# Feed-forward: the gated product goes to a spare PSUM bank, ScalarE writes its high part, VectorE its low part

## The chip, the cores and the metric

One core of a Trainium2 chip runs the whole program. Its engines run side by side and meet only through semaphores: TensorE (PE in the profile, its weight loads PEld), VectorE (DVE), ScalarE (ACT), GpSimd (POOL) and SyncE (SP), which issues most DMAs. SBUF is the memory that all engines read and write. PSUM has eight banks of 128 x 512 fp32 values; matmuls write there. The metric is the time of one execution on the device in microseconds (us), the median of several runs; lower is better.

## The reference

Two layers on 1024 tokens of width 1024, in float32. Each layer is a mixer (convolution and retention in layer 0, stick-breaking attention in layer 1) and a SwiGLU feed-forward, each behind a modulated RMS norm. The change touches the feed-forward alone:

```python
def swiglu(h, w_gate, w_up, w_down):          # w_gate, w_up: 1024 x 2816, w_down: 2816 x 1024
    return (jax.nn.silu(h @ w_gate) * (h @ w_up)) @ w_down

h = rms_norm(x, norm_ffn_g[l]) * (1 + sc2) + sh2
x = x + g2 * swiglu(h, ffn_w_gate[l], ffn_w_up[l], ffn_w_down[l])
```

## The kernel before

Every float32 product is made from two parts. A value is split into a high part (rounded to the type fp32r) and a low part (the value minus the high part), and `three` (lines 566, 571, 572) issues three matmuls: high by high, high by low, low by high. GpSimd splits the weights: per slab of 512 KB four `tensor_scalar` (L544) write the high part and four `tensor_tensor` (L548) the low part. The split of the activations is the work of VectorE, with ScalarE for the norms.

**The feed-forward** is done in 11 chunks (`CHUNKS`) of 256 hidden columns, once as phase `ffn0` (about 640 to 1395 us of the trace) and once as `ffn1` (about 2020 to 2730 us). Tokens are in two halves h of 512, hidden columns in two blocks f of 128. For each h, PE makes four steps of 24 matmuls, gate and up of f = 0 and gate and up of f = 1, into the four banks of `psG` in turn. Then it makes, for each h, eight down steps m of 6 matmuls, again into the four banks in turn. In `ffn0` a chunk ends with eight small matmuls (L617) for the modulation of layer 1.

**The hidden block (h, f)**, called `hidden(h, f)` here, comes between. ScalarE writes `sil`, the SiLU of the gate bank (L950, as all its activations). VectorE multiplies it with the up bank into `hid32` in SBUF (L1547; the trace calls it `hid`). Then `split` makes the high part by a copy with a cast (L1269, `hid_hi`) and the low part by a subtraction (L1271, `hid_lo`). In `ffn0`, `ada` follows after each hidden block: two more VectorE instructions of 128x512 (mostly L1283) that add up the next layer's modulation from a DMA'd piece of `ada_w`. After the last hidden block of a chunk, VectorE takes the 16 down steps: each is one instruction (L1563) that adds a bank of `psG` into `xT`, and so frees the bank.

**What orders it.** There is no scheduler: each engine's program is written out by hand, and the waits are on counters. Two of them matter. The down step m = 4 of half 0 writes the bank of m = 0, so it waits until VectorE's first L1563 has read that. The down steps of half 1 need `f_lo` of `hidden(1, 1)`. The last chunk of `ffn0` (`last_turn`) is written in another order, since the next norm begins in it: the gate and up of (h, f) = (1, 1) come after the down steps of half 0, VectorE does the norm's Newton step (L1320 to L1326) before `hidden(1, 1)`, and PE runs the f = 0 part of four down steps before it waits for `f_lo` of `hidden(1, 1)`.

`psO`, the bank that the change uses, holds the attention outputs in the mixer phases and is otherwise unused in the feed-forward, until the last chunk of `ffn1` turns the output there.

Of the kernel before, what the change touches and what calls it, by code (L numbers as in the profile page):

```python
# [21 lines left out]
F32 = mybir.dt.float32  # L22
F32R = mybir.dt.float32r
ALU = mybir.AluOpType
ACT = mybir.ActivationFunctionType
# [5 lines left out]
H = 512  # L31
# [16 lines left out]
SIL = 2  # L48
# [82 lines left out]
def build(nc, a):  # L131
# [4 lines left out]
    with ExitStack() as ctx:  # L136
# [4 lines left out]
        def at(name, off, shape, dt=F32):  # L141
            return nc.alloc_sbuf_tensor_at(name, [P] + shape, dt, offset=base + off)
# [35 lines left out]
        hid = [at("hid_hi", QO, [2, T], F32R), at("hid_lo", QO + 8 * KB, [2, T], F32R)]  # L178
        F0 = QO + 16 * KB
        sil = [at(f"sil{n}", F0 + 2 * KB * n, [H]) for n in range(SIL)]  # L180
        hid32 = at("hid32", F0 + 4 * KB, [H])
        ada_raw = [at(f"ada_raw{n}", QO + (37 + 4 * n) * KB, [KT // ADA_PIECES, ADA_COLS]) for n in range(2)]
        ada_acc = at("ada_acc", QO + 45 * KB, [4, P])

# [104 lines left out]
        r_ocp = sem("r_ocp")  # L289
        r_rs = sem("r_rs")  # L290
        r_on = sem("r_on")
        f_hi = [sem("f_hi0"), sem("f_hi1")]
        f_lo = [sem("f_lo0"), sem("f_lo1")]
        s_raw_cp = sem("s_raw_cp")
# [24 lines left out]
        def bank(phase, s):  # L319
            return s % PHASE_BANKS.get(phase, BANKS)  # L320
# [6 lines left out]
        def bank_wait(eng, phase, i, s):  # L327

            eng.wait_ge(bank_read[bank(phase, s)], uses(phase, i, s) + 1)
# [11 lines left out]
        def half(h):  # L341
            return slice(H * h, H * h + H)
# [61 lines left out]
        def final(i):  # L404
            return isinstance(i, int) and i == CHUNKS - 1
# [537 lines left out]
        def _(act):  # L943
# [5 lines left out]
            def fn(o, i_, f, **kw):  # L949
                return nc.scalar.activation(o, i_, f, **kw)  # L950

            def load_set(n):
                nc.scalar.add_instruction(mybir.InstLoadActFuncSet(name=nc.get_next_instruction_name(), act_func_set_id=n))
# [9 lines left out]
            def norm_squares(norm, h, x_wait, tiles_after=lambda m: ()):  # L963
                g = 2 * int(norm[-1]) + h
                for k in range(KT):
                    x_wait(h, k)
                    if KT * g + k >= 2:
                        act.wait_ge(n_add, KT * g + k - 1)
                    fn(n_sq[k % 2][:], xT[:, k, half(h)], ACT.Square).then_inc(n_sqd, 1)
                    for tile in tiles_after(k):  # L970
                        norm_hi(norm, 0, tile)

            def norm_root(norm, h):

                g = 2 * int(norm[-1]) + h
                act.wait_ge(misc_done, norm_misc(norm, h))
                if h:
                    act.wait_ge(n_ht, KT * g)
                fn(n_r[:], psM[:], ACT.Ln, bias=EPS).then_inc(n_rs, 1)
                act.wait_ge(n_rs, 2 * g + 1)  # L980
                fn(n_r[:], n_r[:], ACT.Exp, scale=-0.5).then_inc(n_rs, 1)
# [2 lines left out]
                norm_squares(norm, 0, x_wait)  # L984
                norm_second(norm, x_wait, lambda m: NORM_PLAN[1, m][1])

            def norm_second(norm, x_wait, tiles_after, after_squares=None, between=None):
                norm_root(norm, 0)
                norm_squares(norm, 1, x_wait, tiles_after)
                if after_squares:  # L990
                    after_squares()
                norm_root(norm, 1)
                for k in range(KT):
                    norm_hi(norm, 1, k)
                    if between and k == 3:
                        between()
# [84 lines left out]
            def reload(l, stg, x_free):  # L1081


                for n in range(16):
# [10 lines left out]
                    if n in (4, 11):  # L1095
# [2 lines left out]
                        m = 0 if n == 4 else 4  # L1098
                        act.dma_start(xT[:, m:m + 4], x_dram[m:m + 4].rearrange("k p t -> p k t")).then_inc(x_back, 16)

            def ffn_act(phase, squares=None):
                l = int(phase[-1])
                def body(i):
                    for h in range(NH):
                        for f in range(2):
                            s = gu_step(phase, i, h, 2 * f)
                            if squares and final(i) and (h, f) == (1, 1):
                                squares()
                            act.wait_ge(gemm_done, G(phase, i, s))

                            act.wait_ge(f_hi[l], 4 * i + (2 * h + f + 1))
                            fn(sil[f][:], psG[:, bank(phase, s)], ACT.Silu).then_inc(bank_read[bank(phase, s)], 1)
                load_set(SILU_SET)
                chunks(act, body)

# [11 lines left out]
            def qkv_first(phase, i, off, e, head):  # L1127

                hd = head[0] + i * head[1]
                s = 2 * off + e  # L1130
                act.wait_ge(gemm_done, G(phase, i, s))
                m, h, n = qkv_step(phase, e)
                if m < 2:

                    act.wait_ge(s_qk3, hd * 12 + 3 * n)
                    fn(s_raw[:], psG[:, bank(phase, s)], ACT.Copy).then_inc(bank_read[bank(phase, s)], 1)
                    bank_wait(act, phase, i, s)
                    fn(s_sq[:], s_raw[:], ACT.Square).then_inc(s_raw_cp, 1)
                else:

                    act.wait_ge(misc_done, M(phase, i, s) - 1)
                    fn(s_vsb[:], psG[:, bank(phase, s)], ACT.Copy).then_inc(bank_read[bank(phase, s)], 1)
# [64 lines left out]
            def head(phase, i, off, hd, hd_next, par):  # L1207
# [9 lines left out]
                for t in range(1, NT):  # L1217
# [2 lines left out]

            act.sem_inc(s_we, ZRING)
            norm_second("norm2", x_done, lambda m: FINAL_TILES.get(m, ()), lambda: spill("norm2", lambda: None),
                        lambda: qkv_first("qkv0", 0, 0, 0, (0, 0)))
            for e in range(6):
                if e:
                    qkv_first("qkv0", 0, 0, e, (0, 0))
# [29 lines left out]
        def _(dve):  # L1256
# [3 lines left out]
                dve.sem_inc(q, ONE)  # L1260
            dve.sem_inc(s_wst, 3)
            dve.sem_inc(s_wm, 2)
            dve.sem_inc(f_hi[0], SIL)
            dve.sem_inc(f_hi[1], SIL)
            dve.sem_inc(s_spb, 2)

            def split(o, i_, hi_sem, hi_n, lo_sem, add=None):
# [268 lines left out]
            def ffn_dve(phase, norm=None, gains=None):  # L1536
                l = int(phase[-1])
                def body(i):
                    last_one = bool(norm) and final(i)
                    def hidden(h, f):  # L1540
                            e = 2 * h + f
                            n = 4 * i + e
                            s = gu_step(phase, i, h, 2 * f + 1)
                            dve.wait_ge(gemm_done, G(phase, i, s))
                            bank_wait(dve, phase, i, s - 1)
                            dve.wait_ge(f_lo[l], ONE + n)
                            V.tensor_tensor(hid32[:], sil[f][:], psG[:, bank(phase, s)], ALU.mult).then_inc(bank_read[bank(phase, s)], 1)  # L1547
                            bank_wait(dve, phase, i, s)
                            split([q[:, f, half(h)] for q in hid], hid32[:], f_hi[l], n + 1 + SIL, f_lo[l])
                            if phase == "ffn0" and not final(i):  # L1550
                                ada(phase, i, e)
                    for h, f in ((0, 0), (0, 1), (1, 0)):
                        hidden(h, f)
                    if not last_one:
                        hidden(1, 1)
                    for h in range(NH):
                        for m in range(KT):
                            s = down_step(phase, i, h, m)
                            b = bank(phase, s)
                            dve.wait_ge(gemm_done, G(phase, i, s))  # L1560
                            if (h, m) == (1, KT - 1):
                                dve.sem_inc(slab_used, 1)
                            V.scalar_tensor_tensor(xT[:, m, half(h)], psG[:, b], mod[:, l * MOD + 5 * KT + m:l * MOD + 5 * KT + m + 1],  # L1563
                                                   xT[:, m, half(h)], ALU.mult, ALU.add).then_inc(bank_read[b], 1)
                            if last_one:
                                if m >= 2:
                                    norm.add(h, m - 2)
                                if h == 1:
                                    for k in FINAL_TILES.get(m, ()):
                                        norm.h_tile(0, k)  # L1570
                        if last_one:
                            norm.add(h, KT - 2)
                            if h == 0:
                                norm.add(0, KT - 1)
                                gains()
                                norm.newton(0)
                                hidden(1, 1)
                        if phase == "ffn0" and h == 1 and not final(i):
                            ada_cols(phase, i, 0, ada_cols_of(phase, i, 0))
                chunks(dve, body)  # L1580
                if norm:
                    norm.rest()
# [154 lines left out]
```

## Time and profile before

| | us |
|---|---|
| median of 3 runs | 2750.29 |
| lowest, highest | 2749.25, 2760.8 |
| span of the profiled execution | 2751.8 |
| PE busy | 2578.5 (94%) |
| DVE busy | 1377.9 (50%) |
| ACT busy | 543.2 (20%) |
| POOL busy | 973.7 (35%) |

The span is that of one profiled execution, from its first to its last instruction. Durations below come from it. A row of the timeline gives start, duration, engine, line, operation, what it writes and reads, and in brackets the idle time of the engine ahead of it with what ended that. Where rows of one kind follow each other they are merged, "x4" being four of them; a merged row's time runs from the first start to the last end. Since a VectorE instruction starts a little before the one ahead of it is through, starts are the better measure where instructions follow each other closely.

### The profile page before, as it was taken

How to read it: one execution, taken by the hardware profiler on the slowest of the kernel's cores; microseconds unless marked ns; L12 is line 12 of the kernel's file. 1: busy time of each engine (PE TensorE's matmuls, PEld its weight loads, DVE VectorE, ACT ScalarE, POOL GpSimd, SP SyncE). 2: the span in 40 equal slices, each digit the busy share in tenths (PEclk: the TensorE clock that was granted, in tenths of full speed). 3: DMA queues.
4: the chain of work that ended last, by engine and by line, in shares of the span. 5: the costliest groups of instructions: out<-in, count | busy, mean ns of one | idle time of the engine just before them, and what ended most of it. 6: DMA issues, size and time to landing. Idle time of an engine off the chain costs nothing.

```text
span 2751.8 us, 34959 instructions
## 1 busy us (share of the span) xinstructions
PE 2578.5 (94%) x11394; PEld 2103.1 (76%) x11394; DVE 1377.9 (50%) x2143; ACT 543.2 (20%) x987; POOL 973.7 (35%) x1604
## 2 busy tenths in 40 slices
PE   2999888599999999999989999997999999999999
PEld 2787777478888878887858888885778888888887
DVE  5636666546444444444367677777463333332223
ACT  3200111112000000000146666664120000000001
POOL 0432222514444434444322222224064433444430
PEclk7899999899999999999999999997999999999999
DMA  7233333431222222222120111113221111111111
GB/s 277 80 105 97 92 98 107 128 110 62 85 76 83 88 65 79 86 79 69 39 86 26 44 31 43 31 39 105 75 62 54 47 52 46 46 46 53 47 36 61
DMA packets 216925, 201.88 MB, mean 73 GB/s; under 512 B 5994, under 2 KB 165892, under 8 KB 216708
## 3 DMA queue, kind: packets, MB, share of 16 engines
q1 hardware_dynamic: 202708, 164.13, 19.5%
q10 hardware_dynamic: 14128, 36.70, 3.7%
q8 instruction: 38, 0.62, 0.1%
q14 instruction: 51, 0.42, 0.0%
HBM read 179.84 MB, written 20.97 MB: 73 GB/s over the span
## 4 chain that ended last, share of the span: by engine, by line
PE 84%; DVE 9%; DMA 3%; issue 2%; ACT 1%; POOL 1%; SPq 0%; DVEq 0%; ACTq 0%; POOLq 0%
PE psG L566 25%; PE psG L571 25%; PE psG L572 25%; PE psM L819 1%; DVE n_t L1344 1%; PE psG L860 1%; DMA o_stg<-o_spill 1%; PE psO L566 1%; DVE h_lo L1336 1%; PE psZ L849 1%; DMA w_raw<-in_ev_w_in 1%; DVE r_w L1497 1%; PE psO L571 1%; PE psO L572 1%; DVE r_wp L1271 1%
## 5 line engine op out<-in xcount | busy, mean ns | idle before, releaser
L566 PE MATMUL psG<-h_hi,w_split 128*128 128x512 f32 x2496 | 993.5, 398 | 52.1 <-DVE h_lo L1271 33.6
L571 PE MATMUL psG<-h_lo,w_split 128*128 128x512 f32 x2496 | 981.7, 393 | 0.0
L572 PE MATMUL psG<-h_hi,w_split 128*128 128x512 f32 x2496 | 980.8, 393 | 0.0
L544 POOL TENSOR_SCALAR w_split<-w_raw 128x256 fp32r<-128x256 f32 x800 | 368.8, 487 | 1703.5 <-PE psG L566 554.2
L548 POOL TENSOR_TENSOR w_split<-w_raw,w_split 128x256 fp32r<-128x256 f32 x800 | 613.1, 797 | 0.0
L566 PEld LDWEIGHTS psG<-h_hi,w_split 128*128 128x128 f32 x2496 | 474.6, 190 | 169.8 <-issue 34.4
L572 PEld LDWEIGHTS psG<-h_hi,w_split 128*128 128x128 f32 x2496 | 474.3, 190 | 101.2
L571 PEld LDWEIGHTS psG<-h_lo,w_split 128*128 128x128 f32 x2496 | 475.4, 190 | 97.8 <-issue 2.4
L1547 DVE TENSOR_TENSOR hid<-sil,psG 128x512 f32<-128x512 f32 x88 | 60.6, 688 | 720.4 <-PE psG L572 717.8
L1563 DVE SCALAR_TENSOR_TENSOR xT<-psG,mod,xT 128x512 f32<-128x512 f32 x352 | 259.7, 748 | 171.6 <-PE psG L572 171.4
L950 ACT ACTIVATE sil<-psG 128x512 f32<-128x512 f32 x88 | 52.5, 599 | 1307.1 <-PE psG L572 1307.1
L566 PE MATMUL psG<-hid_hi,w_split 128*128 128x512 f32 x704 | 276.6, 393 | 10.1 <-DVE xT L1563 9.9
L571 PE MATMUL psG<-hid_lo,w_split 128*128 128x512 f32 x704 | 275.4, 391 | 0.0
L572 PE MATMUL psG<-hid_hi,w_split 128*128 128x512 f32 x704 | 275.4, 391 | 0.0
L566 PEld LDWEIGHTS psG<-hid_hi,w_split 128*128 128x128 f32 x704 | 133.1, 189 | 40.4 <-issue 13.0
L572 PEld LDWEIGHTS psG<-hid_hi,w_split 128*128 128x128 f32 x704 | 133.0, 189 | 27.9
L571 PEld LDWEIGHTS psG<-hid_lo,w_split 128*128 128x128 f32 x704 | 133.1, 189 | 27.3
L1283 DVE SCALAR_TENSOR_TENSOR ada_acc<-ada_raw,c_act,ada_acc 128x512 f32<-128x512 f32 x140 | 116.0, 829 | 2.8
L950 ACT ACTIVATE s_z<-s_z 128x128 f32<-128x128 f32 (+2 forms) x192 | 100.8, 525 | 6.1
L950 ACT ACTIVATE n_sq<-xT 128x512 f32<-128x512 f32 x64 | 39.9, 630 | 192.6 <-DVE xT L1532 89.6
L1271 DVE TENSOR_TENSOR hid_lo<-hid,hid_hi 128x512 fp32r<-128x512 f32 x88 | 68.2, 775 | 3.0
L1271 DVE TENSOR_TENSOR s_w<-s_w,s_w 128x128 fp32r<-128x128 f32 (+2 forms) x96 | 64.1, 668 | 3.3
(160 smaller groups left out, 2103.2 us busy)
## 6 DMA issues: line engine op xcount, KB each, us to landing
ada_raw<-in_ada_w SPq DMA_DIRECT2D x80, 512.0 KB, 4.0
w_raw<-in_ffn_w_gate SPq DMA_DIRECT2D x44, 512.0 KB, 3.9
w_raw<-in_ffn_w_up SPq DMA_DIRECT2D x44, 512.0 KB, 3.9
w_raw<-in_ffn_w_down SPq DMA_DIRECT2D x44, 512.0 KB, 3.5
w_raw<-in_ev_w_in SPq DMA_DIRECT2D x28, 512.0 KB, 5.1
w_raw<-in_od_w_qkv SPq DMA_DIRECT2D x24, 512.0 KB, 3.8
ada_first<-in_ada_w SPq DMA_DIRECT2D x4, 2048.0 KB, 13.0
x_spill<-xT ACTq DMA_DIRECT2D x2, 4096.0 KB, 16.2
```

The lines of the kernel that those rows point to most:

```text
L544: nc.gpsimd.tensor_scalar(slot[:, 0, part], raw[:, part], 1.0, 1.0, ALU.mult, ALU.mult).then_inc(hi_done, 1)
L548: lo = nc.gpsimd.tensor_tensor(slot[:, 1, part], raw[:, part], slot[:, 0, part].bitcast(F32), ALU.subtract)
L566: mm = nc.tensor.matmul(o, st[0], mv[0], start=first, stop=False, **kw)
L571: nc.tensor.matmul(o, st[0], mv[1], start=False, stop=False, **kw)
L572: return nc.tensor.matmul(o, st[1], mv[0], start=False, stop=end, **kw)
L819: misc(phase, i, 2 * off + e, [lambda: nc.tensor.matmul(psM[:], ones_head, s_sq[:], start=True, stop=True)])
L849: mm = nc.tensor.matmul(zbank[t % ZRING][:, c0:], split_c[:, 1], s_s[:, t % SRING, n, c0:], start=False, stop=n == 1, skip_group_check=True)
L950: return nc.scalar.activation(o, i_, f, **kw)
L1271: V.tensor_tensor(o[1], i_, o[0].bitcast(F32), ALU.subtract).then_inc(lo_sem, 1)
L1283: V.scalar_tensor_tensor(acc, src, cc, acc, ALU.mult, ALU.add).then_inc(ada_step, 1)
L1547: V.tensor_tensor(hid32[:], sil[f][:], psG[:, bank(phase, s)], ALU.mult).then_inc(bank_read[bank(phase, s)], 1)
L1563: V.scalar_tensor_tensor(xT[:, m, half(h)], psG[:, b], mod[:, l * MOD + 5 * KT + m:l * MOD + 5 * KT + m + 1], xT[:, m, half(h)], ALU.mult, ...
```

## The change

The product is written to `psO` instead of `hid32`. ScalarE reads `psO` and writes the high part `hid[0]` with an activation of type Copy. VectorE waits for that and subtracts the high part from `psO`. The cast of VectorE and the buffer `hid32` are gone. A new pair of semaphores, `f_mul`, tells ScalarE of the product. The release of the up bank of `psG`, which the product gave itself, is now a semaphore instruction of VectorE after its wait for the high part. In the last turn of `ffn0`, ScalarE's copy of block (1, 1) stands after the two activations of the norm's root, since VectorE's product stands after the Newton step there. This holds for all 88 hidden blocks of both phases.

```diff
-        hid32 = at("hid32", F0 + 4 * KB, [H])
...
+        f_mul = [sem("f_mul0"), sem("f_mul1")]
...
                 norm_root(norm, 0)
+                if after_root:
+                    after_root()
...
+            def hid_high(l, i, h, f):
+
+                act.wait_ge(f_mul[l], 4 * i + (2 * h + f + 1))
+                fn(hid[0][:, f, half(h)], psO[:], ACT.Copy).then_inc(f_hi[l], 1)
+
...
                             act.wait_ge(gemm_done, G(phase, i, s))
-
-                            act.wait_ge(f_hi[l], 4 * i + (2 * h + f + 1))
                             fn(sil[f][:], psG[:, bank(phase, s)], ACT.Silu).then_inc(bank_read[bank(phase, s)], 1)
+                            if not (squares and final(i) and (h, f) == (1, 1)):
+                                hid_high(l, i, h, f)
...
-                        lambda: qkv_first("qkv0", 0, 0, 0, (0, 0)))
+                        lambda: qkv_first("qkv0", 0, 0, 0, (0, 0)), lambda: hid_high(0, CHUNKS - 1, 1, 1))
...
-            dve.sem_inc(f_hi[0], SIL)
-            dve.sem_inc(f_hi[1], SIL)
...
-                            V.tensor_tensor(hid32[:], sil[f][:], psG[:, bank(phase, s)], ALU.mult).then_inc(bank_read[bank(phase, s)], 1)
-                            bank_wait(dve, phase, i, s)
-                            split([q[:, f, half(h)] for q in hid], hid32[:], f_hi[l], n + 1 + SIL, f_lo[l])
+                            V.tensor_tensor(psO[:], sil[f][:], psG[:, bank(phase, s)], ALU.mult).then_inc(f_mul[l], 1)
+                            dve.wait_ge(f_hi[l], n + 1)
+                            dve.sem_inc(bank_read[bank(phase, s)], 1)
+                            V.tensor_tensor(hid[1][:, f, half(h)], psO[:], hid[0][:, f, half(h)].bitcast(F32), ALU.subtract).then_inc(f_lo[l], 1)
```

VectorE in the loop over the chunks of `ffn0`, the second hidden block of a chunk with its two `ada` instructions. Before:

```order
481 L1547 TENSOR_TENSOR hid_86<-sil_85,psG 128x512 [waits f_lo0]
482 L1269 CAST hid_hi<-hid_86 128x512 [waits bank_read3]
483 L1270 REGISTER_ALU
484 L1271 TENSOR_TENSOR hid_lo<-hid_86,hid_hi 128x512 [waits f_hi0]
485 L1282 ISA [waits ada_in1]
486 L1283 SCALAR_TENSOR_TENSOR ada_acc<-ada_raw_88,c_act,ada_acc 128x512 [waits ada_step]
```

After:

```order
475 L1552 TENSOR_TENSOR psO<-sil_85,psG 128x512 [waits f_lo0]
476 L1555 TENSOR_TENSOR hid_lo<-psO,hid_hi 128x512 [waits f_hi0]
477 L1287 ISA [waits ada_in1]
478 L1288 SCALAR_TENSOR_TENSOR ada_acc<-ada_raw_87,c_act,ada_acc 128x512 [waits ada_step]
479 L1287 REGISTER_ALU
```

The cast is gone, and the subtraction's wait for `f_hi0` is now one for ScalarE. (Lines behind the edit move by five to seven: L1283 becomes L1288.)

ScalarE in the last turn of `ffn0`, from the SiLU of block (1, 1) to the squares of the norm's second half. Before:

```order
195 L950 ACTIVATE sil_85<-psG 128x512 [waits f_hi0,gemm_done]
196 L953 ACT_TABLE_LOAD
197 L950 ACTIVATE n_r<-psM 128x512 [waits misc_done]
198 L950 ACTIVATE n_r<-n_r 128x512 [waits n_rs]
199 L950 ACTIVATE n_sq_76<-xT 128x512 [waits n_add,bank_read0]
```

After:

```order
206 L950 ACTIVATE sil_85<-psG 128x512 [waits gemm_done]
207 L953 ACT_TABLE_LOAD
208 L950 ACTIVATE n_r<-psM 128x512 [waits misc_done]
209 L950 ACTIVATE n_r<-n_r 128x512 [waits n_rs]
210 L950 ACTIVATE hid_hi<-psO 128x512 [waits f_mul0]
211 L950 ACTIVATE n_sq_76<-xT 128x512 [waits n_add,bank_read0]
```

The copy stands between the norm's root and the next squares, and everything of ScalarE behind it waits for VectorE's product.

## Rows read from the trace of the kernel before

**Rows 1.** The page, part 1: busy time, share of the span, instructions.
```profile
PE 2578.5 (94%) x11394; PEld 2103.1 (76%) x11394; DVE 1377.9 (50%) x2143; ACT 543.2 (20%) x987; POOL 973.7 (35%) x1604
```
**Rows 2.** By stretch: us, busy PE PEld DVE ACT POOL, granted clock, DMA share, GB/s.
```profile
1030.00:1033.00 3.00, 3.00 (x9) 2.35 (x8) 1.82 (x3) 0.00 (x0) 0.00 (x0) 0.51 0.94 294
2050.00:2725.00 675.00, 675.00 (x2980) 558.92 (x2979) 202.15 (x292) 24.57 (x41) 267.81 (x475) 1.00 0.15 45
```
**Rows 3.** Waits of PE, 700 to 1360 us: total us, times, longest.
```profile
PE psG L566 <- DVE xT L1563: 9.9, 3, 4.7
```
**Rows 4.** Chain that ended last, 700 to 1360 us: start, us, what.
```profile
708.57 0.79 PE psM L617 x8
...
908.38 0.79 PE psM L617 x8
...
974.61 0.79 PE psM L617 x8
...
1019.84 6.42 DVE hid_hi L1269
...
1047.45 0.79 PE psM L617 x8
...
1320.28 0.79 PE psM L617 x8
```
**Rows 5.** Timeline of DVE in the chunk that ends at 1047 us.
```profile
1019.12 0.69 DVE L1547 TENSOR_TENSOR hid<-sil,psG 128x512 f32<-128x512 f32 x1 [5.80 <-PE psG L572]
...
1026.29 0.69 DVE L1271 TENSOR_TENSOR hid_lo<-hid,hid_hi 128x512 fp32r<-128x512 f32 x1
1026.90 1.53 DVE L1283 SCALAR_TENSOR_TENSOR ada_acc<-ada_raw,c_act,ada_acc 128x512 f32<-128x512 f32 x2
1028.35 2.72 DVE L1563 SCALAR_TENSOR_TENSOR xT<-psG,mod,xT 128x512 f32<-128x512 f32 x4
```
**Rows 6.** Timeline of POOL there.
```profile
1023.17 2.80 POOL L548 TENSOR_TENSOR w_split<-w_raw,w_split 128x256 fp32r<-128x256 f32 x4
```
**Rows 7.** By tile, `hid`: duration in ns, min/median/max.
```profile
L1547 DVE TENSOR_TENSOR hid<-sil,psG x88: 682/689/691, 664.8 to 2716.5; 128x512 f32<-128x512 f32 x88
L1269 DVE CAST hid_hi<-hid x88: 426/428/6414, 665.5 to 2717.2; 128x512 fp32r<-128x512 f32 x88
```
**Rows 8.** By line, the nearest instructions to the new ones, min/median/max in ns.
```profile
L950 ACT ACTIVATE s_v<-psM x16: 597/599/600, 1430.8 to 1869.7; 128x512 fp32r<-128x512 f32 x16
...
L1611 DVE TENSOR_TENSOR s_v<-psM,s_v x16: 679/691/693, 1431.4 to 1870.7; 128x512 fp32r<-128x512 f32 x16
```
**Rows 9.** Timelines of ACT and DVE, a result that passes from ACT to DVE.
```profile
1403.12 0.63 ACT L950 ACTIVATE n_r<-n_r 128x512 f32<-128x512 f32 x1
...
1403.79 0.69 DVE L1320 SCALAR_TENSOR_TENSOR n_t<-psM,n_r 128x512 f32<-128x512 f32 x1 [2.51 <-ACT n_r L950]
```
**Rows 10.** Timelines of DVE and PE, chunks of `ffn0` without a long stall.
```profile
811.09 2.37 DVE L1283 SCALAR_TENSOR_TENSOR ada_acc<-ada_raw,c_act,ada_acc 128x512 f32<-128x512 f32 x2
...
952.89 0.69 DVE L1547 TENSOR_TENSOR hid<-sil,psG 128x512 f32<-128x512 f32 x1 [6.17 <-PE psG L572]
...
957.04 3.40 DVE L1563 SCALAR_TENSOR_TENSOR xT<-psG,mod,xT 128x512 f32<-128x512 f32 x5
...
1091.96 0.69 DVE L1547 TENSOR_TENSOR hid<-sil,psG 128x512 f32<-128x512 f32 x1 [6.04 <-PE psG L572]
...
1096.60 3.37 DVE L1563 SCALAR_TENSOR_TENSOR xT<-psG,mod,xT 128x512 f32<-128x512 f32 x5
...
1097.46 0.49 PE L566 MATMUL psG<-hid_hi,w_split 128*128 128x512 f32 x1
```
**Rows 11.** Timelines of DVE and PE in the last turn of `ffn0`.
```profile
1376.99 0.69 DVE L1547 TENSOR_TENSOR hid<-sil,psG 128x512 f32<-128x512 f32 x1
...
1378.17 0.69 DVE L1271 TENSOR_TENSOR hid_lo<-hid,hid_hi 128x512 fp32r<-128x512 f32 x1
...
1379.10 0.39 PE L566 MATMUL psG<-hid_hi,w_split 128*128 128x512 f32 x1
```

More of the change, by code:

```diff
@@ L985, in norm_act, with norm_second @@
                 norm_second(norm, x_wait, lambda m: NORM_PLAN[1, m][1])
-            def norm_second(norm, x_wait, tiles_after, after_squares=None, between=None):
+            def norm_second(norm, x_wait, tiles_after, after_squares=None, between=None, after_root=None):
                 norm_root(norm, 0)
+                if after_root:
+                    after_root()
                 norm_squares(norm, 1, x_wait, tiles_after)
```

## The prediction, made before the change was run

> **What bounds the kernel now.** I read the page's busy times first: PE is busy for 94% of the span, DVE for half [rows 1]. So only what makes PE wait or run slowly counts. In `ffn1` there is nothing to gain: PE is busy for 675.00 of 675.00 us at a granted clock of 1.00 [rows 2], with the same split work of DVE beside it. In `ffn0`, PE waits three times for L1563, 9.9 us in all, at most 4.7 us [rows 3]. The chain of waits says what is behind it: a single cast of `hid_hi` with 6.42 us is on it [rows 4].
>
> One such place in detail. `hidden(1, 1)` starts at 1019.12, and its cast, normally 428 ns [rows 7], takes from 1019.84 to 1026.26 [rows 4]. GpSimd splits weights all that time, and its run of instructions ends at 1023.17 + 2.80 = 1025.97 [rows 6], 0.3 us before the cast does. So the cast waited for a gap in GpSimd's work and got none for six microseconds. The low part, `ada` and the first L1563 come late by as much (1026.29, 1026.90, 1028.35 [rows 5]), and PE, whose fifth down step needs that bank, stands still for 4.7 us, one of the two longest of its three waits (4.7 + 4.7 + 0.5). Its clock then falls: 0.51 from 1030 to 1033 us, 9 matmuls in 3 us [rows 2], which is the lower of its two levels (1.2 of 2.4 GHz).
>
> What all this costs is best read from the length of chunks. Each chunk of `ffn0` ends with eight L617. The chunk from 908.38 to 974.61 took 66.23 us, the one with the stall (974.61 to 1047.45) 72.84 us [rows 4], so that stall costs 6.6 us: 4.7 of waiting and 1.9 of slow clock. The nine chunks from 708.57 to 1320.28 took 611.71 us [rows 4]; nine of 66.23 would be 596.07. **15.6 us** lie in between: two long stalls, one of half a microsecond, and small ones as at 1097.46, where a first L1563 at 1096.60 was just too late [rows 10].
>
> **The deadline.** In the good chunk the first L1563 starts 957.04 - 952.89 = 4.15 us after the product of `hidden(1, 1)`; in the slightly late one it is 1096.60 - 1091.96 = 4.64 us, and PE starts 0.86 us after that (1097.46) [rows 10]. I put the deadline between the two, at 4.25 us, near the good one.
>
> **Part by part.**
>
> *The cast goes from DVE* (88 times). It is the instruction that waits for GpSimd. The product, which reads one operand from PSUM, never does: 682 to 691 ns in all 88 [rows 7]. Neither does L1611, which subtracts an SBUF operand from PSUM as the new low part will: 679 to 693 ns [rows 8]. So no instruction of a hidden block is left that GpSimd can hold.
>
> The Trainium skill, SBUF — State Buffer, Who interferes with whom, says that a DVE instruction in a two-port mode (a copy or cast in SBUF) and a GpSimd one exclude each other for one whole instruction, and that a DVE instruction with at most one SBUF input outside these modes never contends. The second half agrees with the 682 to 691 ns above; the first half would bound the cast's wait by one GpSimd instruction, and the 6.42 us across several of them do not agree. By it the stalls would be no property of the cast, and the change would bring only the small ones, about 2 us, for about 2748.
>
> *The copy on ScalarE is added* (88 times). The nearest is L950 `s_v<-psM`, a Copy from PSUM to fp32r of the same size: 599 ns [rows 8]. ScalarE is busy for a fifth of the time; the next SiLU comes two PE steps later, so nothing waits behind the copy in a normal chunk. What is queued behind its wait for the product is that SiLU alone.
>
> *The hand-overs.* From ACT to DVE it is 1403.79 - (1403.12 + 0.63) = 0.04 us [rows 9]; I take the same for DVE to ACT.
>
> *The product writes PSUM.* No row shows DVE writing there. The bounds are 0.01 us less than a write to SBUF (679 ns is the least that a product or subtraction of this size took [rows 7, 8]) and one that costs as much again, 0.7 us more. I take the 0.69 us of a write to SBUF, since reading PSUM in place of SBUF changes nothing either (0.69 us for L1271, which reads SBUF twice [rows 5], and 691 ns for L1611 [rows 8]).
>
> The Trainium skill, VectorE: DVE Perf Modes, the section on the TRN2 errata, gives a fixed part of 58 cycles from SBUF and 120 from PSUM, an estimate of 0.065 us more for the new subtraction at 0.96 GHz. It speaks against the change; L1611 at 691 ns does not bear it out. By it the sum would be worse by 0.07 us in the last turn and at most as much in each chunk.
>
> *DVE's time per block.* Before, undisturbed: product to cast 0.72 us (1019.12 to 1019.84 [rows 4, 5]), the cast 0.43 and a gap of 0.03, and `ada` 0.61 us after the low part's start (1026.29 to 1026.90 [rows 5]), 1.79 us in all. After: 0.69 + 0.04 + 0.60 + 0.04 = 1.37 us to the low part, and `ada` at 1.98 us. A pair of `ada` instructions is held by GpSimd as before. Free of it, it lasts 1.53 us, at most 2.37 us [rows 5, 10], and the next instruction starts 0.08 us before its end (1026.90 + 1.53 to 1028.35), so the first L1563 comes at 1.98 + 1.45 = 3.43 us at best and at 1.98 + 2.29 = 4.27 us at the worst. That is at the deadline, so each chunk can lose at most some 0.02 us. The up bank is now released after the copy, some 0.7 us later; the tightest case is that of `hidden(1, 1)`, whose bank PE next needs three down steps (18 matmuls) later, which hides it. In `ffn1` there is no `ada`, and 2.3 us are spare.
>
> *Nine chunks:* -15.6 us, or -14.7 if each keeps 0.1 us. I take **-15.4**.
>
> *The last turn of `ffn0`.* Here the chain is short. Before: product at 1376.99, low part at 1378.17 with its end at 1378.86, and PE starts the f = 1 parts at 1379.10 [rows 11], when its f = 0 parts run out. After: the low part starts at 1376.99 + 1.37 = 1378.36 and ends 0.19 us later than before. PE had no slack worth counting, so **+0.2 us**, which the norm behind it inherits. ScalarE's squares stand behind the copy, but they wait for down steps that end only after 1379, and so lose nothing. If the PSUM write costs 0.7 more, this is +0.9.
>
> *First chunks.* ScalarE comes late out of the norm there, and its second SiLU now also waits for the first product and copy, some 1.4 us. PE needs that bank only two steps (11 us) later. Nothing.
>
> *What takes the place.* With the stalls gone, PE is at its matmuls' own pace, 66.2 us a chunk, as in `ffn1`. Nothing else is near.
>
> **Sum.** -15.4 + 0.2 = -15.2 us on the profiled execution's own 2751.8, so 2736.6. The median of the runs is 1.5 us below the span, which leaves less than one long stall of difference, so I take the same saving there: **2735.1**, or 0.55% less.
>
> **Rivals.**
>
> *One stall was luck.* Whether a cast slips in between GpSimd's instructions is decided by fractions of a microsecond: of nine chunks two show the long stall. If the median run holds only one, the saving is 15.2 - 6.6 = 8.6 us: 2741.7. For it: the runs differ by 11 us (2749.25 to 2760.8), more than a stall. Against: two of the three are within 1.5 us of the profile. It would also come out near there if the `tensor_scalar` that opens `ada` once a chunk, an SBUF to SBUF instruction like the cast, catches one stall of its own. 30%.
>
> *The stalls stay.* GpSimd then holds `ada` or something else as long, and the time is 2748 to 2750. Against: the pair of `ada` never took over 2.37 us. 8%.
>
> *The hand-over is longer, the slower side.* Each hidden block now goes DVE, ACT, DVE, and PE waits for the first L1563 in ten chunks of `ffn0`. With a delay D beyond my 1.37 us, each chunk loses D minus 0.3 us (a room between the 0 and 0.8 us above). The 15.4 us are eaten at D = 1.8, and the kernel is over 0.5% slower at D = 3.2 (10 x 2.9 = 29 us, less 15.2). At D = 3.2 that is 2764, and with D minus 2.3 us in each of 11 chunks of `ffn1`, 10 us more, 2774. Against: both instructions and the hand-over have near rows; only the PSUM write has none, and it would have to take several times as long. 5%. With D of 0.7, the upper bound of the write, the loss is 4 us in the chunks and 0.7 in the last turn: 2739.8. 7%.
>
> **How the numbers follow.** The forecast has 50%, the lucky stall 30%, D near 0.7 7%, stalls that stay 8%, slower 5%. About 0.5% (13.8 us, to 2736.5) is what a measurement can tell from no change, and the forecast lies only 1.4 us beyond it. Faster by over 0.5%: most of the forecast and nothing else, 49%. Within: 46%. Slower: 5%. The range goes from 2731 (a median run of before with part of a stall more than the profile) to 2745 (one stall and D of 0.7 together); the forecast's own range is 2733 to 2738.
>
> **What the profile would show.** No cast of `hid_hi` on DVE, no wait of PE for the down step's addition (L1563 before), no granted clock near 0.5 in `ffn0`; chunks of 66.2 to 66.4 us between the groups of eight small matmuls; ScalarE's copy at 0.60 us, the product at 0.69, the low part at 0.69 with 0.7 us ahead of it; PE starting its f = 1 parts 0.2 us late in the last turn. I am wrong if the product's write to PSUM is slow, if `ada` takes over the stalls, or if later phases shift against GpSimd by more than they gain.

## The result, and the profile after

| | before | changed |
|---|---|---|
| median of 18 runs each | 2761.61 us | 2770.81 us |
| lowest, highest | 2740.78, 2769.14 | 2761.21, 2780.16 |
| span of the profiled execution | 2751.8 | 2767.9 |

The ratio is 1.0048 with a 95% interval of 1.0028 to 1.0069. The change makes the kernel half a percent slower here, where 0.55% faster was forecast. Two things in this table matter for what follows. The median of the kernel before is 11 us above that of the three runs shown ahead of the prediction, which are the first three of these 18, and its runs spread over 28 us. Of the experiments below, one run of e2 fell in a slow state, 3751.74 us at a mean granted clock of 0.649, and its ratio leaves that run out.

Where did the time go? The profile after, PE's waits in `ffn0` (700 to 1375 us; total us, times, longest), for [rows 3]:

```profile
PE psG L566 <- DVE xT L1569: 17.7, 7, 2.8
```

Three waits, 9.9 us in all, have become seven, 17.7 us in all. The chain of waits, 640 to 1400 us, for [rows 4]:

```profile
711.26 0.79 PE psM L617 x8
755.86 0.71 DVE psO L1552
756.59 0.61 ACT hid_hi L950
757.94 4.11 DVE ada_acc L1288
...
781.65 0.79 PE psM L617 x8
...
991.76 0.79 PE psM L617 x8
1057.99 0.79 PE psM L617 x8
...
1334.96 0.79 PE psM L617 x8
```

No cast is on the chain any more. Instead it goes through the product, ScalarE's copy, and then 4.11 us of a single `ada` instruction. That chunk (711.26 to 781.65) takes 70.39 us, one without a stall (991.76 to 1057.99) still 66.23. The nine chunks take 623.70 us in place of 611.71, which is 12.0 of the 16.1 us between the two spans. Another 2.7 us lie ahead of the first chunk's end (711.26 against 708.57), where the thirteen traces of this case differ by up to 9.5 us, those of one and the same kernel before by 6.0; 1.5 us lie behind the last chunk.

The tiles of the new instructions, duration in ns, min/median/max, for [rows 7, 8], and `ada` under them:

```profile
L1552 DVE TENSOR_TENSOR psO<-sil,psG x88: 687/696/697, 667.5 to 2732.6; 128x512 f32<-128x512 f32 x88
L950 ACT ACTIVATE hid_hi<-psO x88: 597/599/602, 668.2 to 2733.3; 128x512 fp32r<-128x512 f32 x88
L1555 DVE TENSOR_TENSOR hid_lo<-psO,hid_hi x88: 690/692/694, 669.0 to 2734.0; 128x512 fp32r<-128x512 f32 x88
...
L1288 DVE SCALAR_TENSOR_TENSOR ada_acc<-ada_raw,c_act,ada_acc x140: 740/752/4498, 107.8 to 1316.3; 128x512 f32<-128x512 f32 x140
```

Everything that the change adds runs as forecast, all 88 times: nothing of a hidden block is held by GpSimd any more. But `ada`, with both its tensor operands in SBUF, now reaches 4498 ns. The timelines of DVE and of POOL in the first stalled chunk, for [rows 5, 6]:

```profile
755.86 0.70 DVE L1552 TENSOR_TENSOR psO<-sil,psG 128x512 f32<-128x512 f32 x1 [6.69 <-PE psG L572]
757.33 0.69 DVE L1555 TENSOR_TENSOR hid_lo<-psO,hid_hi 128x512 fp32r<-128x512 f32 x1 [0.78 <-ACT hid_hi L950]
757.94 4.88 DVE L1288 SCALAR_TENSOR_TENSOR ada_acc<-ada_raw,c_act,ada_acc 128x512 f32<-128x512 f32 x2
```

```profile
757.19 1.51 POOL L544 TENSOR_SCALAR w_split<-w_raw 128x256 fp32r<-128x256 f32 x4
758.67 2.82 POOL L548 TENSOR_TENSOR w_split<-w_raw,w_split 128x256 fp32r<-128x256 f32 x4
```

`ada` comes 0.75 us into GpSimd's last slab of the run and ends its first instruction at 757.94 + 4.11 = 762.05, 0.56 us after the run's end at 758.67 + 2.82 = 761.49. It waited through all that was left of the slab, as the cast did in [rows 4, 6]. In a chunk where nothing is lost, DVE comes at nearly the same point:

```profile
1036.36 0.70 DVE L1552 TENSOR_TENSOR psO<-sil,psG 128x512 f32<-128x512 f32 x1 [6.63 <-PE psG L572]
1037.83 0.69 DVE L1555 TENSOR_TENSOR hid_lo<-psO,hid_hi 128x512 fp32r<-128x512 f32 x1 [0.78 <-ACT hid_hi L950]
1038.44 1.80 DVE L1288 SCALAR_TENSOR_TENSOR ada_acc<-ada_raw,c_act,ada_acc 128x512 f32<-128x512 f32 x2
```

```profile
1037.75 1.96 POOL L544 TENSOR_SCALAR w_split<-w_raw 128x256 fp32r<-128x256 f32 x4
```

Here `ada` comes 0.69 us into the slab, gets in (the pair takes 1.80 us), and it is GpSimd that is held up: 1.96 us for four L544 in place of 1.51. The place in the slab does not decide it. In the same trace another `ada` also comes 0.69 us into a slab (1244.77 - 1244.08), and its pair takes 4.96 us:

```profile
1244.77 4.96 DVE L1288 SCALAR_TENSOR_TENSOR ada_acc<-ada_raw,c_act,ada_acc 128x512 f32<-128x512 f32 x2
```

```profile
1244.08 1.53 POOL L544 TENSOR_SCALAR w_split<-w_raw 128x256 fp32r<-128x256 f32 x4
1245.55 2.84 POOL L548 TENSOR_TENSOR w_split<-w_raw,w_split 128x256 fp32r<-128x256 f32 x4
```

### The profile page after: what moved, and what is told of

Its sections match the earlier page's. It is cut to its first block, busy times and chain, and to the rows that moved or that the text cites. A ratio compares the mean times of both kernels' runs of the same rounds, so it can differ in the third digit from the quotient of the medians.

```text
span 2767.9 us, 34966 instructions
## 1 busy us (share of the span) xinstructions
PE 2587.8 (93%) x11394; PEld 2109.9 (76%) x11394; DVE 1330.8 (48%) x2055; ACT 596.3 (22%) x1075; POOL 946.7 (34%) x1604
## 4 chain that ended last, share of the span: by engine, by line
PE 84%; DVE 9%; DMA 3%; issue 2%; ACT 1%; POOL 1%; DVEq 0%; SPq 0%; ACTq 0%; POOLq 0%
PE psG L566 25%; PE psG L571 25%; PE psG L572 25%; DVE ada_acc L1288 2%; PE psM L819 1%; DMA o_stg<-o_spill 1%; PE psG L860 1%; PE psZ L849 1%; PE psO L566 1%; DVE n_t L1349 1%; DMA w_raw<-in_ev_w_in 1%; DVE r_w L1502 1%; DVE h_lo L1341 1%; PE psO L571 1%; PE psO L572 1%
## 5 line engine op out<-in xcount | busy, mean ns | idle before, releaser
L544 POOL TENSOR_SCALAR w_split<-w_raw 128x256 fp32r<-128x256 f32 x800 | 348.2, 463 | 1746.6 <-PE psG L566 560.9
L1552 DVE TENSOR_TENSOR psO<-sil,psG 128x512 f32<-128x512 f32 x88 | 61.3, 696 | 713.9 <-PE psG L572 711.3
L1569 DVE SCALAR_TENSOR_TENSOR xT<-psG,mod,xT 128x512 f32<-128x512 f32 x352 | 259.9, 749 | 174.8 <-PE psG L572 174.7
L566 PE MATMUL psG<-hid_hi,w_split 128*128 128x512 f32 x704 | 278.7, 396 | 17.7 <-DVE xT L1569 17.7
L950 ACT ACTIVATE hid_hi<-psO 128x512 fp32r<-128x512 f32 x88 | 52.8, 600 | 483.4 <-DVE psO L1552 483.4
L1288 DVE SCALAR_TENSOR_TENSOR ada_acc<-ada_raw,c_act,ada_acc 128x512 f32<-128x512 f32 x140 | 137.5, 982 | 2.8
L1555 DVE TENSOR_TENSOR hid_lo<-psO,hid_hi 128x512 fp32r<-128x512 f32 x88 | 60.9, 692 | 68.7 <-ACT hid_hi L950 68.7
```

Of the source, the lines that this page charges most:

```text
L544: nc.gpsimd.tensor_scalar(slot[:, 0, part], raw[:, part], 1.0, 1.0, ALU.mult, ALU.mult).then_inc(hi_done, 1)
L566: mm = nc.tensor.matmul(o, st[0], mv[0], start=first, stop=False, **kw)
L1288: V.scalar_tensor_tensor(acc, src, cc, acc, ALU.mult, ALU.add).then_inc(ada_step, 1)
L1552: V.tensor_tensor(psO[:], sil[f][:], psG[:, bank(phase, s)], ALU.mult).then_inc(f_mul[l], 1)
L1555: V.tensor_tensor(hid[1][:, f, half(h)], psO[:], hid[0][:, f, half(h)].bitcast(F32), ALU.subtract).then_inc(f_lo[l], 1)
```

## The experiments

**Theory A:** The stall belongs to no one instruction. Any VectorE instruction that has two operands in SBUF, or that copies within SBUF, can be caught by GpSimd's run of split instructions; the change takes the cast out of the row and leaves `ada` as the next to be caught. **Rival B:** the way over ScalarE makes VectorE late, and `ada` only shows it. **Rival C:** with `ada` out of the way, the change pays as forecast.

The length of the nine chunks of `ffn0` between the first and the last group of L617 is the measure: without a stall it is 596.1 us. The median of the kernel before was 2749.5 us beside e1 to e4 and 2748.5 beside e5 to e8. Those two groups and e9 to e11 ran on three different chips; which chip the first table comes from is not on record.

**e1: the changed kernel with `ada` adding up in PSUM.**

```diff
-                acc = ada_acc[:].rearrange("p k c -> p (k c)")
+                acc = psZ[:, 0] if phase == "ffn0" else ada_acc[:].rearrange("p k c -> p (k c)")
...
+                    dst = ada_acc[:].rearrange("p k c -> p (k c)") if kt == KT - 1 else acc
...
-                        V.scalar_tensor_tensor(acc, src, cc, acc, ALU.mult, ALU.add).then_inc(ada_step, 1)
+                        V.scalar_tensor_tensor(dst, src, cc, acc, ALU.mult, ALU.add).then_inc(ada_step, 1)
```

> Edit: the changed kernel, but in ffn0 the modulation sum ada_acc is kept in an idle PSUM bank (psZ) while it is added up, and only its last instruction writes the SBUF tile that PE reads. Nothing of the computation is left out. Theory A: in the changed kernel the stalls moved from the cast to the next VectorE instruction with two operands in SBUF, ada (L1288, up to 4498 ns, a pair up to 5.29 us), because it comes while GpSimd works through a slab. With ada_acc in PSUM ada has one SBUF operand, like L1552 and L1555, which never took over 0.70 us; so ada stays at about 0.75 us each, PE has no wait for xT, the nine chunks of ffn0 take 596 to 599 us in place of 623.7, and the time is some 25 us under the changed kernel's 2770.8 median: 2740 to 2748. Rival B: the hand-over to ScalarE makes VectorE late by itself, and ada only shows what was late: then the nine chunks stay above 610 us and the time at 2762 or more.

Measured: median 2737.8 us, 0.9962 of the kernel before (0.9941 to 0.9983). Its chain of waits, ends of the first and last of the nine chunks, and the tile `psZ` (ns, min/median/max):

```profile
711.15 0.79 PE psM L617 x8
...
1307.25 0.79 PE psM L617 x8
```

```profile
L1289 DVE SCALAR_TENSOR_TENSOR psZ<-ada_raw,c_act,psZ x60: 745/752/757, 670.2 to 1287.7; 128x512 f32<-128x512 f32 x60
```

596.10 us, and these 60 `ada` instructions, which read and write the sum in PSUM, never take over 757 ns. The hand-over to ScalarE is in this kernel as in the changed one, so rival B falls. The time lies 2 us below the expected 2740 to 2748, and that of e3 3 us.

**e2: the kernel before with the same edit to `ada`.**

> Edit: the same move of ada_acc to PSUM in ffn0, in the kernel before. Nothing is left out. Beside e1 it gives the change under study with ada out of the way. Theory A: the cast (L1269) still has its stalls, some of them of 6 us, but ada and its contention are gone, so the nine chunks of ffn0 lie between 596 and 612 us, and the time is a few us below the kernel before and 0 to 12 us above e1. Rival C: the long stalls of the cast depend on what ada did to GpSimd's order, and are as likely without it: then no gain, within 3 us of the kernel before.

Measured: median 2737.41 us, 0.9966 (0.994 to 0.9991), nine chunks 596.09 us. It is as fast as e1. The 2x2 of e1, e2 and the two kernels says that with `ada` out of the way the change is worth nothing: rival C, the forecast's core, falls too. The tile `hid_hi` of e2:

```profile
L1269 DVE CAST hid_hi<-hid x88: 426/428/1042, 665.2 to 2699.6; 128x512 fp32r<-128x512 f32 x88
```

In this trace the cast was never caught for long, and up to 1.04 us of it is covered, since two `ada` instructions that are never held leave room.

**e3: the changed kernel with the last `ada` of a chunk ahead of `hidden(1, 1)`.**

```diff
-                            if phase == "ffn0" and not final(i):
+                            if phase == "ffn0" and not final(i) and e < 3:
                                 ada(phase, i, e)
+                                if e == 2:
+                                    ada(phase, i, 3)
```

> Edit: the changed kernel, but the fourth ada piece of a chunk stands before hidden(1, 1), right behind the third, in the 6.7 us in which VectorE is idle there. Nothing is left out. Theory A: ada may still be held by GpSimd for some us, but now between two hidden blocks, where 6.7 us of idle time cover it; behind hidden(1, 1) only instructions with one SBUF operand are left, so PE does not wait: nine chunks of ffn0 at 596 to 600 us, time 2740 to 2748. Rival B (hand-over): L1552 of hidden(1, 1) to the first xT would still be late, no gain over the changed kernel's 2770.8 of more than 6 us.

Measured: median 2736.97 us, 0.9962 (0.9945 to 0.9979), nine chunks 596.10 us. `ada` keeps its SBUF operands here; only its place is another. So it is `ada` behind the last hidden block that makes PE wait.

**e4: ScalarE's part undone, the product still in PSUM.**

```diff
-                            if not (squares and final(i) and (h, f) == (1, 1)):
-                                hid_high(l, i, h, f)
...
+                            dve.wait_ge(f_mul[l], n + 1)
+                            V.tensor_copy(hid[0][:, f, half(h)], psO[:]).then_inc(f_hi[l], 1)
```

> Edit: the changed kernel with ScalarE's part undone: the product goes to psO, and VectorE itself makes the high part by a copy from psO and then the low part. Nothing is left out. No VectorE instruction of a hidden block has two SBUF operands or copies from SBUF, and ada begins some 2.1 us after the product, as in the changed kernel (2.09 us there). Theory A: it is ada that is caught, so it is caught here too: pairs of 4 to 5 us in several chunks, nine chunks of ffn0 at 610 to 630 us, time within 8 us of the changed kernel's 2770.8. Rival B (ScalarE's hand-over is the cause): no stalls of that kind, chunks of about 66.5 us, time 2740 to 2750.

Measured: median 2748.16 us, ratio 1.0007 (0.9985 to 1.0028); nine chunks in its trace 615.73 us (711.99 to 1327.72). Its chain:

```profile
1022.27 0.70 DVE hid_hi L1553
1023.72 4.11 DVE ada_acc L1287
...
1301.36 0.70 DVE hid_hi L1553
1302.81 5.13 DVE ada_acc L1287
...
1327.72 0.79 PE psM L617 x8
```

The mechanism is as theory A has it: without ScalarE, `ada` is caught all the same, in four of ten chunks. The expected time, within 8 us of 2770.8, was missed by 15 us, and the measured one lies where rival B expected it (2740 to 2750). It is the trace that speaks against B, not the time; and the traced execution is the slowest of the ten (2763.39 us). In e8 the changed kernel itself is as fast.

**e5: gaps in GpSimd's work.** In `ffn0` it writes high and low part of each quarter in turn, each low part waiting for the high part just issued.

```diff
+                            if phase == "ffn0":
+                                high(q)
                             part = slice(q * D // QUARTERS, (q + 1) * D // QUARTERS)
                             pool.wait_ge(hi_done, QUARTERS * n + (q + 1))
```

> Edit: the changed kernel, but in ffn0 GpSimd writes the high and the low part of each quarter in turn, and each low part waits for the high part just issued, so GpSimd's instructions no longer follow each other without a gap. ada stays as it is, with two SBUF operands. Nothing is left out. Theory A1: VectorE gets past GpSimd only where GpSimd's row of instructions has a gap; in the changed kernel it has none inside a slab, so ada waits up to 4.5 us. With a gap every quarter it waits at most for one pair, 1.2 us: no pair of ada over 3.5 us, nine chunks of ffn0 at 596 to 602 us, time 2737 to 2743. Theory A2: it is not the gaps but chance at each instruction's end: stalls of 2 to 5 us stay in some chunks, nine chunks at 604 or more.

Measured: median 2738.52 us, 0.9956 (0.9935 to 0.9977), nine chunks 596.16 us. POOL's timeline shows the gaps, and `ada_acc` by tile how long `ada` takes:

```profile
749.41 0.74 POOL L553 TENSOR_TENSOR w_split<-w_raw,w_split 128x256 fp32r<-128x256 f32 x1
750.12 0.40 POOL L544 TENSOR_SCALAR w_split<-w_raw 128x256 fp32r<-128x256 f32 x1
750.60 1.18 POOL L553 TENSOR_TENSOR w_split<-w_raw,w_split 128x256 fp32r<-128x256 f32 x1
```

```profile
L1293 DVE SCALAR_TENSOR_TENSOR ada_acc<-ada_raw,c_act,ada_acc x140: 740/752/1285, 106.4 to 1281.1; 128x512 f32<-128x512 f32 x140
```

L544 ends at 750.52 and L553 starts at 750.60: 0.08 us between the two, where before each instruction started ahead of the other's end. `ada` gets its turn within a quarter, and none takes over 1.29 us any more. The operands and the place of `ada` are those of the changed kernel.

That the gap does this is not shown, though, since e5 also changes the order of GpSimd's instructions. The longest `ada` got in where there is no gap, between a low part and the next high part:

```profile
882.91 2.09 DVE L1293 SCALAR_TENSOR_TENSOR ada_acc<-ada_raw,c_act,ada_acc 128x512 f32<-128x512 f32 x2
```

```profile
882.91 0.74 POOL L553 TENSOR_TENSOR w_split<-w_raw,w_split 128x256 fp32r<-128x256 f32 x1
883.62 0.84 POOL L544 TENSOR_SCALAR w_split<-w_raw 128x256 fp32r<-128x256 f32 x1
```

It waited for the one low part, and L544, which starts 0.03 us before that one's end, was then held up to 0.84 us. Three of the ten `ada` behind `hidden(1, 1)` went this way. Whether the gap or the order ends the long waits was not tried apart.

**e6: the kernel before with the last `ada` ahead of `hidden(1, 1)`.**

> Edit: the kernel before, with the fourth ada piece of a chunk moved ahead of hidden(1, 1), as e3 does for the changed kernel. Nothing is left out. With e3 it gives the change under study with ada out from behind hidden(1, 1), but with two SBUF operands as before. The cast of hidden(1, 1) can still be held, but 1.5 us more of it are covered. Theory A: cast stalls of 6 us in none to two chunks, nine chunks 596 to 608 us, time 2736 to 2746, never better than e3's 2737.0 by over 2 us. Rival C (the change helps where ada is out of the way): 5 us or more slower than e3.

Measured: median 2737.35 us, 0.9958 (0.9925 to 0.999), nine chunks 596.10 us, the longest cast 1029 ns. It is within 0.4 us of e3: a second 2x2 in which the change brings nothing.

**e7: GpSimd's instructions of `ffn0` cut to 8 of 256 columns.**

> Edit: the changed kernel, but in ffn0 each of GpSimd's split instructions writes only 8 of its 256 columns, so the weights of ffn0 are mostly stale: this part of the split is left out, and the output is not the reference's. Everything else, ada with its two SBUF operands too, is as in the changed kernel. Theory A: without GpSimd's work ada takes 0.75 us each (a pair 1.53), no stall, nine chunks of ffn0 at 596 us, time 2735 to 2741. Rival B (hand-over, or the DMAs into ada's buffers): stalls stay.

Measured: median 2738.28 us, 0.997 (0.9945 to 0.9995), nine chunks 596.10 us. With GpSimd's work nearly taken away, the stalls are gone: behind `hidden(1, 1)` no `ada` takes over 0.78 us. It is also no faster than e1, e3, e5 and e6: once nobody is caught, sharing with GpSimd costs this kernel nothing.

**e8 to e11: both kernels again, for their traces.**

> Edit: none, the changed kernel as it is, on the same chip as e5 to e7. The time of this kernel and of the one before goes with the number of chunks in which ada or the cast is caught. Expected: 12 to 25 us over e5, between the same and 1% slower than the kernel before, and in its profile two to seven pairs of ada of 4.5 us or more behind hidden(1, 1).

> Edit: none, the kernel before once more, for its trace. Theory A: a caught cast or ada is a matter of chance chunk by chunk, and its count sets the span. Expected: none to three casts over 5 us in ten chunks of ffn0, and a span that is 2734 us plus the excess of the chunks over 66.23 us each, to within 6 us.

> Edit: none, the changed kernel once more, for its trace. Theory A: two to seven of ten pairs of ada behind hidden(1, 1) of 4.8 us or more, each such chunk 69 to 76 us long, and a span that is 2734 us plus the excess of the chunks over 66.23 us each, to within 6 us. None of the pairs between 2.4 and 4.8 us, since a caught ada waits to the end of GpSimd's run.

> Edit: none, the kernel before a third time, for its trace: as for e9.

| trace | caught, of ten chunks | nine chunks, us | span, us |
|---|---|---|---|
| before | 2 casts | 611.71 | 2751.8 |
| e9, before | 3 casts | 614.69 | 2748.3 |
| e11, before | 0 | 597.13 | 2735.5 |
| changed | 7 ada | 623.70 | 2767.9 |
| e8, changed | 3 ada | 614.15 | 2755.6 |
| e10, changed | 6 ada | 622.12 | 2763.3 |

Caught means over 4 us for the one instruction; casts of up to 1.95 us are not counted. A caught cast costs its chunk 5.6 to 7.0 us over 66.23 (e9: 72.03, 72.03 and 71.83 us), a caught `ada` 2.7 to 4.8. At the end of e8 and e10 it is 9.3 and 9.1 us: there `ada` comes in GpSimd's fourth slab and gets in only behind the fifth (timeline of DVE, e10):

```profile
1303.08 9.12 DVE L1288 SCALAR_TENSOR_TENSOR ada_acc<-ada_raw,c_act,ada_acc 128x512 f32<-128x512 f32 x2
1312.12 2.06 DVE L1569 SCALAR_TENSOR_TENSOR xT<-psG,mod,xT 128x512 f32<-128x512 f32 x3
```

The spans of e9 to e11 are within 4.4 us of 2734 us plus the excess of their chunks, as expected.

All 21 caught instructions of these traces ended at the same point: 0.28 us (a cast) or 0.55 us (an `ada`) after the last instruction of a slab. In three of them (ends at 1298.45 in before, 1303.75 in e8, 1311.40 in e10) GpSimd went on with another slab at once. So they did not wait for the end of GpSimd's whole run. Nor is the end of a slab a sure way in, since all five casts and two of the `ada` had already passed one.

Over all six traces 5 of 30 casts were caught in the kernel before, and 16 of 30 `ada` in the changed one. Each one costs less, but three times as many are caught. e8 was timed too: 2749.26 us, ratio 1.0007 (0.9977 to 1.0037). So beside e5 to e7 the same change that cost 0.48% above cost nothing, and e8 lies 10.7 us over e5, where 12 to 25 were expected. The changed kernel's two medians lie 21.5 us apart; at 2.7 to 4.8 us each that would be five to eight more caught `ada` per execution, by estimate. Those of the kernel before lie 13.1 us apart, about two caught casts. The traces show that the number differs from execution to execution. What shifts its mean between one set of runs and another is open; the chip is one candidate.

## Why the prediction was wrong

**The bound of the kernel and the deadline: right.** PE is bound by itself except in `ffn0`, where it waits for VectorE's first addition. In `ffn1` it is busy for 664.00 of 664.00 us in the changed kernel. The undisturbed chunk is 66.23 us in every trace. The slow clock behind a stall showed again: 0.66 granted on the mean from 834 to 839 us. In the chunks of the changed kernel with nobody caught, the first L1569 comes 3.55 to 3.89 us after the product, and the chunk takes 66.23 us, as reckoned.

**The price of each new instruction: right.** Product 0.70 us, copy 0.60, subtraction 0.69. DVE writes PSUM for 7 ns more than SBUF (696 against 689), so the rival of the slow hand-over had no ground. From product to low part it is 1.47 us where 1.37 was reckoned, and `ada` begins at 2.08 us in place of 1.98, since the way back takes longer than the 0.04 us of [rows 9]. ScalarE starts 0.03 us after the product's end, but VectorE's low part 0.14 us after the copy's end: the wait now stands at the semaphore instruction that gives back the bank, and the low part only behind it.

**The last turn of `ffn0`: right.** From the product to the first addition it is 1394.90 - 1391.67 = 3.23 us, before 1379.98 - 1376.99 = 2.99: +0.24 for +0.2. In e1, as in the changed kernel (at 1393.11 and 1393.89 us), PE waits twice there (PE's weight loads):

```profile
1365.40 0.19 PEld L566 LDWEIGHTS psG<-hid_hi,w_split 128*128 128x128 f32 x1 [0.27 <-DVEq L1555]
1366.18 0.19 PEld L566 LDWEIGHTS psG<-hid_hi,w_split 128*128 128x128 f32 x1 [0.26 <-DVE hid_lo L1556]
```

The first wait is for the bank, which VectorE's semaphore instruction now gives back only after the copy. The prediction had found that release hidden everywhere. Here it is not, but it adds nothing to the sum, since PE then waits for the low part all the same.

**The step that failed** is the sentence "A pair of `ada` instructions is held by GpSimd as before", with its bound of 2.37 us. That bound was read from chunks in which `ada` came right behind a cast and a low part that had already got in between GpSimd's instructions. In the kernel before, the long stalls fell on the cast, which comes first, and neither the low part nor `ada` took over 1.23 us. With the cast gone and the low part reading PSUM, `ada` is first, and nothing in the rows bounded it then: a caught pair took 4.9 to 5.3 us in the changed kernel's trace, where at most 2.37 was reckoned, and 9.3 us in e8. The rival "the stalls stay" named this case, but gave it 8% and the old number of stalls; in the trace there were seven in place of two.

The Trainium skill, SBUF — State Buffer, Who interferes with whom, says that a VectorE instruction with two SBUF inputs contends with a GpSimd instruction that reads SBUF. That names `ada`, and the traces agree: 757 ns at most with one SBUF input (e1), 4498 with two (the changed kernel). The prediction used the sentence for the instructions that the change adds, and not for those that stay. The page also says that whoever is first holds the shared ports for the whole instruction, while the other blocks. Read as a wait for one instruction, as the prediction reads it, that does not fit: in the changed kernel `ada` waited through six GpSimd instructions (757.94 to 761.49 us).

**The saving of 15.4 us had a wrong base too.** It took the two stalls of one trace as the kernel's. The trace of e11 has none, at 2735.5 us, and the 18 runs of before spread from 2741 to 2769. The rival "one stall was luck" saw this from one side only.

**What is shown and what is open.** Shown: `ada` behind `hidden(1, 1)` is what makes PE wait (e1, e3); GpSimd is what holds it (e7); alternating GpSimd's high and low parts, with 0.08 us ahead of each low part, ends it (e5); ScalarE's part is not the cause (e1, e4). Not shown: which of the two, the order or the gap, does it in e5; why an instruction that comes 0.69 us into a slab gets in once and not another time, why the cast is caught less often than `ada` (5 and 16 of 30), and why it was hardly caught in e2 and e6. The cast comes 0.72 us after the product, often with another slab still ahead, and `ada` at 2.08 us in GpSimd's last one; that would fit, but was not tried apart.

**The versions that beat both kernels** are e1, e2, e3, e5 and e6, at 2737 to 2738.5 us. The simplest is e6: the kernel before, with one `ada` moved into a time when VectorE is idle, 0.42% faster than before. The change under study adds nothing to it.

## What to carry to other kernels

When a VectorE instruction is held up by GpSimd, moving that instruction to another engine can hand the stall to the next one of its kind on VectorE; look down the row for what comes first after the edit, and do not bound it by rows in which it came second. What helped here was to take such work out from behind the deadline (e3, e6), to give it a PSUM operand (e1), and to let GpSimd's high and low parts alternate (e5). And where a trace holds a few rare long stalls, count them over several executions before a saving is built on them.

## What the runs showed of the hardware

- A VectorE instruction with two SBUF operands (e8: 8524 ns) or a cast within SBUF (6414 ns) can wait through many back-to-back GpSimd instructions, not just one: five to fourteen whole ones in the 21 caught cases. Normally they take 752 and 428 ns.
- All 21 ended 0.28 us (cast) or 0.55 us (`ada`) after the last instruction of a slab, three of them while GpSimd went straight on with the next slab.
- With high and low parts alternating and 0.08 us ahead of each low part, `ada` took 1285 ns at most (e5).
- With one operand in PSUM, the same additions took 745 to 757 ns under the same GpSimd work (e1).
- VectorE wrote 128x512 fp32 into PSUM in 696 ns, into SBUF in 689 ns.
